# Up projection of block 2's first layer as 2 by 2 blocks: seven products in place of eight, block sums on VectorE

## What is computed

```python
def conv_ffn_2(h, lp):
    u = h @ lp["w_up"]
    ch = u.shape[-1]
    u = lax.conv_general_dilated(
        u, lp["conv_w"][:, None, :].astype(u.dtype), window_strides=(1,),
        padding=((CONV_W // 2, CONV_W // 2),), dimension_numbers=("NWC", "WIO", "NWC"),
        feature_group_count=ch) + lp["conv_b"]
    a, v = jnp.split(u, 2, axis=-1)
    return (jax.nn.silu(a) * v) @ lp["w_down"]
...
    x = x + gt2 * conv_ffn_2(modulate(x, lp["g_norm2"], sh2, sc2), lp)
    if update_ctx:
        ...
        xc = xc + c_gt2 * conv_ffn_2(modulate(xc, lp["g_norm2"], c_sh2, c_sc2), lp)
```

## Time and profile before

| | us |
|---|---|
| median of three runs | 2732.1 |
| lowest and highest run | 2727.31 and 2736.45 |
| the profiled execution | 2729.41 |
| its span | 2727.4 |
| TensorE busy in the span | 2655.5 |
| VectorE, ScalarE, GpSimd busy | 861.8, 534.3, 298.2 |

### The profile page before, as it was taken

The page is one execution under the profiler, slowest core; times in us unless marked ns, Lnnn a source line. Parts: engine busy times, 40 slices in busy tenths (PEclk is TensorE's granted clock), DMA queues, the critical chain, the costliest instruction groups (busy, mean ns, idle before and its releaser), DMA issues.

```text
span 2727.4 us, 28537 instructions
## 1 busy us (share of the span) xinstructions
PE 2655.5 (97%) x11310; PEld 1971.3 (72%) x11310; DVE 861.8 (32%) x1642; ACT 534.3 (20%) x1063; POOL 298.2 (11%) x280
## 2 busy tenths in 40 slices
PE   7999999999899999999999999999999999999999
PEld 5757888886578888645644448888845875887887
DVE  3024177731324776314700003111100235102220
ACT  1131133111112320212610002111100223102320
POOL 0010111000110110002510000000000004100100
PEclk9989999999899999998999999999999998999999
DMA  5322276833235675110002111212121130233342
GB/s 205 146 93 104 82 298 262 315 115 135 77 124 215 257 277 221 63 68 35 1 35 103 71 62 62 93 62 92 73 85 74 62 133 1 105 135 128 150 177 100
DMA packets 31391, 333.79 MB, mean 122 GB/s; under 512 B 2881, under 2 KB 9153, under 8 KB 9153
## 3 DMA queue, kind: packets, MB, share of 16 engines
q1 hardware_dynamic: 31296, 332.45, 32.3%
HBM read 331.39 MB, written 1.05 MB: 122 GB/s over the span
## 4 chain that ended last, share of the span: by engine, by line
PE 95%; DVE 3%; POOL 1%; ACT 1%; issue 0%; DMA 0%; DVEq 0%; POOLq 0%; ACTq 0%
PE PS L658 28%; PE PS L550 26%; PE PS L2189 9%; PE PS L1152 5%; PE PS L1306 5%; PE PS L2205 5%; PE PS L970 3%; PE PS L1318 2%; PE PS L1786 2%; PE PS L981 2%; PE PS L993 2%; PE PS L428 1%; PE PS L1902 1%; PE PS L2058 1%; PE PS L822 1%; DVE probs_t L503 1%
## 5 line engine op out<-in xcount | busy, mean ns | idle before, releaser
L658 PE MATMUL PS<-XN,slot 128*128 128x256 f32 x3520 | 764.1, 380 | 10.0 <-DVE XN L490 5.1
L658 PEld LDWEIGHTS PS<-XN,slot 128*128 128x128 f32 x3520 | 671.0, 191 | 102.9 <-issue 11.1
L550 PE MATMUL PS<-arena,slot 128*128 128x256 f32 x1824 | 399.8, 381 | 9.8 <-POOL arena L1707 5.5
L550 PEld LDWEIGHTS PS<-arena,slot 128*128 128x128 f32 x1824 | 348.5, 191 | 60.2 <-POOL arena L1707 6.6
L550 PE MATMUL PS<-XN,slot 128*128 128x256 f32 (+1 forms) x1248 | 312.4, 411 | 5.0 <-DVE XN L490 5.0
L752 DVE SCALAR_TENSOR_TENSOR arena<-PS,small,arena 128x255 f32<-128x255 f32 (+2 forms) x352 | 168.5, 539 | 441.5 <-ACT arena L727 441.5
L550 PEld LDWEIGHTS PS<-XN,slot 128*128 128x128 f32 x1248 | 237.7, 191 | 76.7 <-issue 43.0
L2189 PE MATMUL PS<-XN,slot 128*128 128x512 f32 (+1 forms) x768 | 255.5, 486 | 0.0
L2189 PEld LDWEIGHTS PS<-XN,slot 128*128 128x128 f32 x768 | 145.8, 190 | 101.2 <-issue 91.4
L779 POOL TENSOR_TENSOR arena<-arena 128x256 f32 (+3 forms) x88 | 87.4, 994 | 734.9 <-ACT arena L730 734.9
L727 ACT ACTIVATE arena<-PS,small 128x256 f32<-128x256 f32 (+1 forms) x176 | 99.2, 614 | 273.5 <-PE PS L658 272.9
(11 more groups left out here) (195 smaller groups left out, 2126.3 us busy)
## 6 DMA issues: line engine op xcount, KB each, us to landing
slot<-in_weights SPq DMA_DIRECT2D x86, 2048.0 KB, 7.8
arena<-in_mod SPq DMA_DIRECT2D x48, 1024.0 KB, 6.9
slot<-in_weights SPq DMA_DIRECT2D x16, 2816.0 KB, 9.8
slot<-in_weights SPq DMA_DIRECT2D x16, 2304.0 KB, 8.5
slot<-in_weights SPq DMA_DIRECT2D x2, 2176.0 KB, 8.7
slot<-in_weights SPq DMA_DIRECT2D x4, 1024.0 KB, 4.8
small<-in_small SPq DMA_DIRECT2D x1, 2685.0 KB, 19.2
arena<-in_c SPq DMA_DIRECT2D x2, 1024.0 KB, 10.9
```

What stands on the lines that cost most here:

```text
L550: mm = pe.matmul(o, l, r, start=k == 0, stop=k == len(terms) - 1, skip_group_check=True)
L658: mm = pe.matmul(o, slots[slot][:, a:a + P], XN[:, k, seg[g]], start=k == 0, stop=k == DK - 1, skip_group_check=True)
```

## The change

It is switched on for layer `b0` alone. The weights of a tile form 2 by 2 blocks: A11 and A12 are the gate half with even and odd row blocks, A21 and A22 the value half. The right side is B11 and B12 (even row blocks of `XN`, segments 0 and 1) and B21 and B22 (odd ones). Each block product is four products of 128x128 tiles with 256 columns. VectorE forms S1 = A21 + A22, S2 = S1 - A11, S3 = A11 - A21 (in place of A21) and S4 = A12 - S2 for each tile from 1 on, one tile ahead, and once T1 = B12 - B11, T2 = B22 - T1, T3 = B22 - B12 and T4 = T2 - B21. TensorE forms P1 = A11 B11, P2 = A12 B21, P3 = S4 B22, P4 = A22 T4, P5 = S1 T1, P6 = S2 T2 and P7 = S3 T3, where P2 is added to P1 and P3 to P5 in PSUM. The results are block 11 = P1 + P2, U2 = P1 + P6, U3 = U2 + P7, block 12 = U2 + P5 + P3, block 21 = U3 - P4 and block 22 = U3 + P5. VectorE makes the five sums that are not made in PSUM; ScalarE copies P1 (`P1C`) before P2 is added.

Tile 0 keeps its 32 products (banks 0 and 7). A tile's taps, Silu and product of halves run one step later than before, beside the products of the next tile. The loops are now two tiles written out, four turns of four, and four tiles written out; SP's loop follows. S1, S2 and S4 of even tiles lie in an unused part of the slot, those of odd tiles in `PR`; the T sums lie in `SQ`. The diff, its core:

```diff
+SEVEN = ("b0",)
...
 def ffn_stages(s, up, down):
     tiles = []
     for m in range(FM):
-        tiles += down_tiles(up, DK, [m]) + down_tiles(up, DK, [m], col=FF)
+        g, u = down_tiles(up, DK, [m]), down_tiles(up, DK, [m], col=FF)
+        tiles += g[0::2] + g[1::2] + u[0::2] + u[1::2] if s in SEVEN else g + u
...
+        W_FIRST, W_TURNS = 2, 4
+        W_LAST = W_FIRST + PAIRS * W_TURNS
+        P1C, U2, U3, CU = area(13312, T), area(13568, T), area(13824, T), area(14080, 2 * T)
+        TSUM = SQ.rearrange("p a b -> p (a b)").rearrange("p (s k t) -> p s k t", s=4, t=T)
+        WSUM = PR.rearrange("p a b -> p (a b)")[:, 0:12 * P]
+        XQ = XN.rearrange("p (k e) t -> p k e t", e=2)
...
+        def w_steps(eng, body, last):
+            for i in range(W_FIRST):
+                body(i, None, i)
+            with C.loop(eng, 0, W_TURNS) as turn:
+                for p in range(PAIRS):
+                    body(p, turn, turn * PAIRS + W_FIRST + p)
+            for i in range(W_LAST, last):
+                body(i, None, i)
+        def w_sums(slot, odd):
+            sums = WSUM if odd else slots[slot][:, 32 * P:44 * P]
+            return [sums[:, j * 4 * P:(j + 1) * 4 * P] for j in range(3)]
+        def w_quarters(slot, odd):
+            return [slots[slot][:, (16 * odd + 4 * j) * P:(16 * odd + 4 * j + 4) * P] for j in range(4)]
...
+        def tensor_up_seven(pe, s, norm):
...
+            def body(i, turn, m):
+                if turn is None and i == 0:
+                    first(i)
+                    return
+                odd = i % 2
+                slot, landed = w_slab(s, i, turn)
+                a11, a12, s3, a22 = w_quarters(slot, odd)
+                s1, s2, s4 = w_sums(slot, odd)
+                start = turn is None and i == 1
+                if not odd:
+                    pe.wait_ge(sems[f"landed{slot}"], landed)
+                def product(lhs, rhs, bank, first=True, last=True):
+                    for k in range(4):
+                        mm = pe.matmul(PS[:, bank, 0:T], lhs[:, k * P:(k + 1) * P], rhs[:, k, :], start=first and k == 0,
+                                       stop=last and k == 3, skip_group_check=True)
+                    return mm
+                if start:
+                    for b in (1, 2, 3, 4, 5, 6):
+                        claim(pe, b)
+                else:
+                    pe.wait_ge(*w_of(s, "conv", i, turn, 1))
+                product(a11, XQ[:, :, 0, 0:T], odd, last=False).then_inc(*w_tick(s, TD, "p1", i, turn))
+                if start:
+                    pe.wait_ge(*of(s, "sums", "block", 0))
+                    pe.wait_ge(*of(s, "t2"))
+                else:
+                    pe.wait_ge(*w_of(s, "u2", i, turn, 1))
+                product(s2, TSUM[:, 1], 4).then_inc(*w_tick(s, TD, "p6", i, turn))
+                if not start:
+                    pe.wait_ge(*w_of(s, "u3", i, turn, 1))
+                product(s3, TSUM[:, 2], 5).then_inc(*w_tick(s, TD, "p7", i, turn))
+                product(s1, TSUM[:, 0], 2 + odd, last=False).then_inc(*w_tick(s, TD, "p5", i, turn))
+                if start:
+                    pe.wait_ge(*of(s, "t4"))
+                else:
+                    pe.wait_ge(*w_of(s, "c21", i, turn, 1))
+                product(a22, TSUM[:, 3], 6).then_inc(*w_tick(s, TD, "p4", i, turn))
+                pe.wait_ge(*w_of(s, "p1_copied", i, turn))
+                product(a12, XQ[:, :, 1, 0:T], odd, first=False)
+                pe.wait_ge(*w_of(s, "c22", i, turn))
+                product(s4, XQ[:, :, 1, T:2 * T], 2 + odd, first=False).then_inc(*w_tick(s, TD, "p3", i, turn))
+                if odd:
+                    key = ("slab", g0 + (i if turn is None else W_FIRST + i) // 2)
+                    C.found[key] = C.found[(s, "p3", i) if turn is not None else (s, "p3", "block", i)]
+                    if C.open is not None:
+                        C.open.append(key)
+            w_steps(pe, body, FM)
...
+        def scalar_up_seven(act, s):
+            _, _, centre = conv_spec("b", [0, 1])
+            def body(i, turn, m):
+                if turn is None and i == 0:
+                    return
+                start = turn is None and i == 1
+                hb = HB[:, (i - 1) % 2, :, :]
+                src = w_sources(i, turn)
+                if start:
+                    act.wait_ge(*of(s, "p3", "block", 0))
+                else:
+                    if turn is not None or i > 2:
+                        act.wait_ge(*w_of(s, "h", i, turn, 2))
+                    act.wait_ge(*w_of(s, "c21", i, turn, 1))
+                for half in (1, 0):
+                    if half == 0 and not start:
+                        act.wait_ge(*w_of(s, "c12", i, turn))
+                    act.activation(hb[:, half, :], src[half], ACT.Identity, bias=conv_col(s, m - 1, half, 3),
+                                   scale=conv_col(s, m - 1, half, centre))\
+                        .then_inc(*w_tick(s, SD, f"bias{half}", i, turn))
+                if turn is not None or i < FM:
+                    act.wait_ge(*w_of(s, "p1", i, turn))
+                    if not start:
+                        act.wait_ge(*w_of(s, "u2", i, turn, 1))
+                    act.activation(P1C, PS[:, i % 2, 0:T], ACT.Copy).then_inc(*w_tick(s, SD, "p1_copied", i, turn))
+                act.wait_ge(*w_of(s, "conv", i, turn))
+                act.activation(hb[:, 0, :], hb[:, 0, :], ACT.Silu).then_inc(*w_tick(s, SD, "act", i, turn))
+            w_steps(act, body, FM + 1)
...
+        def vector_up_seven(dve, s, norm):
...
+            def weight_sums(i, turn):
+                j = i + 1
+                odd = j % 2
+                slot, landed = w_slab(s, j, turn)
+                a11, a12, a21, a22 = w_quarters(slot, odd)
+                s1, s2, s4 = w_sums(slot, odd)
+                if turn is None and i == 0:
+                    dve.wait_ge(sems[f"landed{slot}"], landed)
+                if not odd:
+                    dve.wait_ge(sems[f"landed{slot}"], landed)
+                if turn is not None or i > 0:
+                    dve.wait_ge(*w_of(s, "p3", i, turn, 1))
+                dve.tensor_tensor(s1, a21, a22, ALU.add).then_inc(*w_tick(s, VD, "s1", i, turn))
+                dve.tensor_tensor(a21, a11, a21, ALU.subtract).then_inc(*w_tick(s, VD, "s3", i, turn))
+                dve.wait_ge(*w_of(s, "s1", i, turn))
+                dve.tensor_tensor(s2, s1, a11, ALU.subtract).then_inc(*w_tick(s, VD, "s2", i, turn))
+                dve.wait_ge(*w_of(s, "s2", i, turn))
+                dve.tensor_tensor(s4, a12, s2, ALU.subtract).then_inc(*w_tick(s, VD, "sums", i, turn))
+            def token_sums():
+                b11, b12, b21, b22 = [XQ[:, :, e, seg[g]] for e in range(2) for g in range(2)]
+                t1, t2, t3, t4 = [TSUM[:, j] for j in range(4)]
+                for g in range(2):
+                    for k in range(DK):
+                        for label in norm(k, g):
+                            dve.wait_ge(*of(*label))
+                dve.tensor_tensor(t1, b12, b11, ALU.subtract).then_inc(*tick(VD, s, "t1"))
+                dve.tensor_tensor(t3, b22, b12, ALU.subtract).then_inc(*tick(VD, s, "t3"))
+                dve.wait_ge(*of(s, "t1"))
+                dve.tensor_tensor(t2, b22, t1, ALU.subtract).then_inc(*tick(VD, s, "t2"))
+                dve.wait_ge(*of(s, "t2"))
+                dve.tensor_tensor(t4, t2, b21, ALU.subtract).then_inc(*tick(VD, s, "t4"))
...
+            def body(i, turn, m):
+                if turn is None and i == 0:
+                    weight_sums(i, turn)
+                    token_sums()
+                    return
+                if turn is not None or i > 1:
+                    dve.wait_ge(*w_of(s, "p3", i, turn, 1))
+                    dve.tensor_tensor(PS[:, (i - 1) % 2, T:2 * T], PS[:, 2 + (i - 1) % 2, 0:T], U2, ALU.add)\
+                        .then_inc(*w_tick(s, VD, "c12", i, turn))
+                if turn is None and i == FM:
+                    tap_steps(i, turn, m)
+                    return
+                if turn is not None or i < FM - 1:
+                    weight_sums(i, turn)
+                dve.wait_ge(*w_of(s, "p6", i, turn))
+                dve.wait_ge(*w_of(s, "p1_copied", i, turn))
+                dve.tensor_tensor(U2, PS[:, 4, 0:T], P1C, ALU.add).then_inc(*w_tick(s, VD, "u2", i, turn))
+                tap_steps(i, turn, m)
+                dve.wait_ge(*w_of(s, "u2", i, turn))
+                dve.wait_ge(*w_of(s, "p7", i, turn))
+                dve.tensor_tensor(U3, PS[:, 5, 0:T], U2, ALU.add).then_inc(*w_tick(s, VD, "u3", i, turn))
+                dve.wait_ge(*w_of(s, "u3", i, turn))
+                dve.wait_ge(*w_of(s, "p5", i, turn))
+                dve.tensor_tensor(CU[:, T:2 * T], PS[:, 2 + i % 2, 0:T], U3, ALU.add)\
+                    .then_inc(*w_tick(s, VD, "c22", i, turn))
+                dve.wait_ge(*w_of(s, "p4", i, turn))
```

(72 more changed lines are left out.)

41 lines of the change are left out of this document (35 added, 6 removed).

## The result

The changed kernel takes 2697.86 us (median of four runs, 2694.87 to 2700.37) against 2729.7 us for the kernel before (four runs by then); the ratio is 0.9879 with a 95% interval of 0.9857 to 0.9901. That is 32 us less, with an interval of 27 to 39 us, where 36 us were forecast. The changed kernel's profiled execution took 2700.37 us.

A forecast was written before the change was run, and what follows sets the result against it. The prediction took the stage to be bound by TensorE's number of products alone. From the median 2732.1 us it took 36.3 and added 0.5, forecasting 2696 us, with an 8 in 10 range of 2688 to 2710.

The forecast's parts named there:

- What bounds the stage, and the price of a product: Block 2's first layer: only the number of TensorE products counts, 0.4317 us each; 84 fewer save 36.3 us.
- No cost for the seven groups and their waits: Changed stage on TensorE: waits and increments every four products add zero, as in the out projection's groups of 8.
- The drained pipe: TensorE's pipe empties at each block product's start, 0.353 us by 147 starts, 52 us, so 2748 us; chance 0.03.
- (d): TensorE's granted clock falls as it cycles through PSUM banks: 36 us given back, or up to 2830 us; chance 0.02.
- VectorE's chain: Inside a tile, the sum of block 22 ends at 8.0 to 8.4 us, asked for at 10.36; reserve 2.0 to 2.4.
- rival (c): VectorE becomes the bound: weight sums of 1.6 to 1.7 us equal the old time, 2 us give 2761; chance 0.02.
- the wait for P6: VectorE's U2 in each tile needs P6, done at 3.45 + 0.2 us, just after the weight sums end at 3.6.
- T2's place at the start: Stage start: T2, third of VectorE's T sums, ready at 1689.7 to 1691.3 us, asked for at 1691.6; 0 to 0.5 us.
- Start and end: Stage edges: T2 in time at the start; at the end GpSimd's last product some 0.7 us later, costing zero.
- SBUF: GpSimd's product hardly falls beside the weight sums; if it did, VectorE would lose 0.5 us of reserve, TensorE nothing.
- The sum: Whole kernel: median 2732.1 less 36.3 plus 0.5 gives 2696.3 us, forecast as 2696; no-stall chance 0.84.
- The 0.5 us for small things: Loop turns and stage start: an added allowance of 0.5 us, bounds 0 to 2 us.

The follow-up runs named there:

- the other order: Against the changed kernel, U3 and the sum of block 22 ahead of the taps: with two products fewer 2625.78 us, with eight more sums 2718.72 us.

## Why the prediction was right

**What bounds the stage, and the price of a product.** Right. The stage took 267.63 us where 267.7 were forecast, with 1240 records at 0.2158 us. TensorE's line has no idle time in it, and one more product left out was worth 35.65 us. The exchange of 32 products for 28 passed through the time one to one.

**No cost for the seven groups and their waits.** Right; the nearest row, groups of eight products, carried over to groups of four. The drained pipe, 52 us, did not occur. The clock stayed 1.00 in the stage while TensorE went through seven groups of products in other banks a tile, so (d) did not occur either. The Trainium skill's section on depth-cycling ("TensorE: Matmul & The Clock Gate", "A second HAM failure mode: psum-queue depth-cycling") ties the loss to micro-idles between groups; the trace of the changed kernel has none, so it neither confirms nor contradicts it. In the run with eight more sums TensorE idled once a tile, 1.3 us by the profile, and its clock was 1.00 from 1712 us on all the same; only its longest wait, 3.4 us, had a stretch of 0.69 behind it.

**VectorE's chain.** The order was right, the size a little pessimistic: the sum of block 22 ended 7.7 us into a tile where 8.0 to 8.4 were forecast, as weight sums that don't depend on each other start 0.60 us apart, where 0.73 were allowed. That this chain is what reaches the time first is shown by four runs: 2.4 us more a tile are free but for the first tile, 4.8 us more cost 35.5, two products fewer cost the wait at that place, and the other order took it away. It is not the only way: with eight more sums in the other order TensorE waited for the taps, and there VectorE's total was the bound. The break-even for rival (c), weight sums of 1.6 to 1.7 us (3.6 to 4.1 us more a tile than 0.69 each), was too low: with 4.8 us more a tile, the time equalled the old one. By the trace it is 12.08 - 7.68 + 0.59 = 5.0 us. The forecast had the end of the chain 0.3 to 0.7 us too late, and the wait for P6, 0.59 us, at 0.1 or less. Neither T2's place at the start nor this chain cost the changed kernel anything, and no engine waited for a slab in the stage (they landed 8.5 us after their issue, by the median of nine, with 12.09 us to do so).

**Start and end.** T2 was to be ready 0.3 to 1.9 us ahead of TensorE. VectorE's T sums and TensorE's P6:

```profile
1690.56 1.22 DVE L968 TENSOR_TENSOR SQ<-XN,SQ 128x1024 f32<-128x1024 f32 x1
...
1694.14 1.89 PE L858 MATMUL PS<-SQ,probs 128*128 128x256 f32 x8
```

Ready at 1691.78, asked for at 1694.14: 2.4 us, since all four T sums took 1.22 us, about as the undisturbed row (1.21). At the end a step failed without cost:

```profile
1950.51 1.27 POOL L1029 TENSOR_TENSOR arena<-arena 128x512 f32<-128x512 f32 x1 [7.65 <-ACT arena L931]
```

GpSimd's last product began 4.1 us behind the stage's end, not 5.8: I added the sum of block 12 and did not see that the value half's bias step, formerly behind the end as well, is now done 2 us before it.

**SBUF.** Right in that it costs nothing here, as GpSimd's product falls where it was expected; wrong in size. I took the 0.5 us of the earlier trace rows as the price. There GpSimd's product was 256 columns wide; the one of this stage is 512, and where it met a sum the sum was 0.95 to 1.07 us longer, with five products up to twice in a tile. The Trainium skill's statement in "GPSIMD Engine Reference", section Specifications, names instructions with two SBUF inputs as the ones that contend; the runs agree, with the sizes above.

**The sum.** 2696 us against 2697.86 and, once more, 2695.85. Part of that closeness is chance: the median of three runs that the sum started from, 2732.1, lay 2 to 3 us above what more runs of the kernel before gave, 2728.9 to 2729.7, and the gain between medians was 32 to 33 us, not 35.8. The term that was right is the stage's. What the sum put at nothing without a row is the rest of the program: behind the stage the same work took 4 us longer in every profile of this stage, with the mean clock of the stretch shown above at 0.81 where it was 0.84, and the gain between medians falls short of 36.3 by the same 3 to 4 us. Why is not shown, and only one profile of the kernel before lies beside them. So the total came out at 2696 because two errors of this size cancelled. The 0.5 us for small things was found nowhere in the stage.

## What to carry to other kernels

Where one engine is busy for a whole stage, a change is worth the work that it takes from that engine, at the price of one record there, as long as every wait put in its way has a reserve; so list the waits, those of the first tile apart, and work out each reserve before anything else. The reserve of the other engine is set by the longest chain back into the bound engine, not by its idle time: with 4.8 us more a tile and 1.76 us still idle VectorE cost the whole gain, and the same work in another order cost two thirds of that, or 5 us once GpSimd kept away from SBUF. Ordering a result that the bound engine asks for ahead of one that it doesn't is the first thing to do when such a reserve runs out. And a gain in one stage is best read from that stage: here 36.25 us went there in each of four profiles, and 4 came back at the low clock 225 us and more behind it.

## What the runs showed of the hardware

A GpSimd product of 128x512 that met an unbroken row of VectorE sums with both inputs in SBUF took 7.54 us in place of 1.27, as long as the row, and ended in the one sum of it that had to wait for the result of the sum just before. VectorE's sum then took 1.64 us in place of 0.69. How far the product came in between, the trace doesn't tell; that it stood still until the row was broken is my reading, and no run varied the row. In the run with five products a tile the delay fell on up to two of the four sums, 1.76 us each. Sums with one input in PSUM, beside the same products, kept their 0.42 us.

A wait of TensorE can cost more than itself. Behind a wait of 2.44 us the granted clock was 0.75 for 6.9 us, with records of up to 635 ns in place of 379 (eight more sums, other order, GpSimd's product nearly gone), and 0.69 for 5.1 us behind one of 3.40 us (eight more sums). But in that same run it stayed 1.00 behind a first wait of 2.44 us and behind 19 of 1.3 us.
